# Early modulation weights on whole rows, write-outs of turned x behind them, and another order of late chunks in the feed-forward head

## The reference

```python
cs  = silu(c)                              # c: one row for the prompt, one for the sample
mod = cs @ w_mod + b_mod                   # w_mod: 2048 x 12288
sh_a, sc_a, gt_a, sh_f, sc_f, gt_f = split(mod, 6)
h = rmsnorm(x, g_attn) * (1 + sc_a) + sh_a
z = h @ w_in                               # queries, keys, values of two groups of heads
o = concat(differential_attention(z), sliding_window_attention_with_sinks(z))
x = x + gt_a * (o @ w_out)
h2 = rmsnorm(x, g_ffn) * (1 + sc_f) + sh_f
u = conv3(h2 @ w_up) + conv_b              # causal, depthwise, w_up: 2048 x 11264
gate, val = split(u, 2)
x = x + gt_f * ((silu(gate) * val) @ w_down)
y = rmsnorm(x, g_final)
```

## Time and profile before

| | |
|---|---|
| median of three runs | 2729.01 us |
| profiled execution | 2726.82 us |
| its span | 2724.7 us |
| PE busy | 2638.6 us, 97% |
| DVE busy | 1632.5 us, 60% |
| ACT busy | 962.2 us, 35% |
| POOL busy | 529.8 us, 19% |
| moved by DMA | 324.93 MB, 307.67 MB of it read from HBM |

### The profile page before, as it was taken

The page is one execution under the profiler, slowest core; times in us unless marked ns, Lnnn a source line. Parts: engine busy times, 40 slices in busy tenths (PEclk is TensorE's granted clock), DMA queues, the critical chain, the costliest instruction groups (busy, mean ns, idle before and its releaser), DMA issues.

```text
span 2724.7 us, 50979 instructions
## 1 busy us (share of the span) xinstructions
PE 2638.6 (97%) x20135; PEld 2462.7 (90%) x20135; DVE 1632.5 (60%) x3210; ACT 962.2 (35%) x1871; POOL 529.8 (19%) x461
## 2 busy tenths in 40 slices
PE   7999999999999999899999999999999999999997
PEld 2258989988988999899999999999999999999997
DVE  1359889884446889865445555545554555455564
ACT  2235666664345335432222222222222222222224
POOL 1037777771012443310000000000000000000003
PEclk9999999999999999999999999999999999999998
DMA  8766555562224654533323222332322233233231
GB/s 277 255 211 180 184 173 183 179 175 63 55 57 136 164 170 136 152 109 94 88 84 94 78 83 89 94 92 80 93 88 78 84 94 93 79 93 91 81 93 69
DMA packets 416208, 324.93 MB, mean 119 GB/s; under 512 B 44410, under 2 KB 360218, under 8 KB 414880
## 3 DMA queue, kind: packets, MB, share of 16 engines
q1 hardware_dynamic: 410032, 302.55, 37.5%
q0 software_dynamic: 5248, 14.56, 1.7%
q10 hardware_dynamic: 688, 4.47, 0.5%
HBM read 307.67 MB, written 14.07 MB: 118 GB/s over the span
## 4 chain that ended last, share of the span: by engine, by line
PE 83%; DVE 7%; DMA 3%; issue 2%; POOL 2%; ACT 2%; SPq 1%; ACTq 0%; DVEq 0%; POOLq 0%
PE ps L1574 24%; PE ps L1576 23%; PE ps L1575 23%; PE ps L1548 4%; DVE late_f L1241 3%; PE ps L1663 2%; PE ps L1629 2%; DMA w_raw<-in_w_out 2%; DMA w_raw<-in_w_mod 1%; POOL oT L699 1%; PE ps L1647 1%; SPq L539 1%; ACT w_hi L795 1%; DVE oT L1241 1%; PE ps L1585 1%
## 5 line engine op out<-in xcount | busy, mean ns | idle before, releaser
L1574 PE MATMUL ps<-x_hi,w_hi 128*128 128x272 f32 (+1 forms) x4480 | 1320.1, 295 | 33.0 <-DVE w_lo L1135 23.7
L1575 PE MATMUL ps<-x_lo,w_hi 128*128 128x272 f32 (+1 forms) x4480 | 1298.1, 290 | 0.0
L1576 PE MATMUL ps<-x_hi,w_lo 128*128 128x272 f32 (+1 forms) x4480 | 1296.1, 289 | 0.0
L1574 PEld LDWEIGHTS ps<-x_hi,w_hi 128*128 128x128 f32 x4480 | 850.5, 190 | 48.2 <-issue 24.1
L1576 PEld LDWEIGHTS ps<-x_hi,w_lo 128*128 128x128 f32 x4480 | 851.9, 190 | 0.0
L1575 PEld LDWEIGHTS ps<-x_lo,w_hi 128*128 128x128 f32 x4480 | 849.6, 190 | 0.0
L795 ACT ACTIVATE w_hi<-w_raw 128x1024 fp32r<-128x1024 f32 x368 | 375.4, 1052 | 1052.0 <-PE ps L1576 904.3
L1135 DVE TENSOR_TENSOR w_lo<-w_raw,w_hi 128x1024 fp32r<-128x1024 f32 x368 | 460.7, 1280 | 344.1 <-ACT w_hi L795 343.7
L1576 PE MATMUL ps<-y_hi,w_lo 128*128 128x272 f32 x1408 | 406.8, 289 | 0.0
L1574 PE MATMUL ps<-y_hi,w_hi 128*128 128x272 f32 x1408 | 406.1, 288 | 0.0
L1575 PE MATMUL ps<-y_lo,w_hi 128*128 128x272 f32 x1408 | 404.5, 287 | 0.0
(11 more groups left out here) (195 smaller groups left out, 2116.7 us busy)
## 6 DMA issues: line engine op xcount, KB each, us to landing
w_raw<-in_w_mod SPq DMA_DIRECT2D x192, 512.0 KB, 4.5
w_raw<-in_w_up SPq DMA_DIRECT2D x176, 512.0 KB, 4.6
w_raw<-in_w_down SPq DMA_DIRECT2D x88, 512.0 KB, 4.0
w_raw<-in_w_in SPq DMA_DIRECT2D x56, 512.0 KB, 3.9
w_raw<-in_w_in SPq DMA_DIRECT2D x32, 256.0 KB, 3.7
w_raw<-in_w_out SPq DMA_DIRECT2D x16, 512.0 KB, 5.4
w_raw<-in_w_out SPq DMA_DIRECT2D x64, 128.0 KB, 4.0
x_transposed<-xT SPq DMA_DIRECT2D x4, 1088.0 KB, 7.3
```

The lines of the kernel that those rows point to most:

```text
L1574: pe.matmul(out[:, 0:n], hi_w, hi_x, start=first, stop=False)
L1575: pe.matmul(out[:, 0:n], hi_w, lo_x, start=False, stop=False)
L1576: return pe.matmul(out[:, 0:n], lo_w, hi_x, start=False, stop=last)
```

## The change

Four things are changed in the first 250 us, and one in the feed-forward head.

1. An early k step is one matmul on all 128 rows into one bank. `mod_rows` has 512 columns instead of 1024, and `group_columns` turns them by four transposes instead of eight accumulating matmuls.
2. The transposes of x use two pairs of banks in turn, so a block waits for the copy of the block two before it. The scaled x goes into a tile of its own, hT, instead of back into xT.
3. The four write-outs of turned x stand behind the early weights in SP's queue: blocks 8 to 15 first, in the middle of the first late chunks and w_in chunks (`X_OUT`). Their semaphore is split in two. VectorE, ScalarE and POOL wait for blocks 8 to 15 at late chunk 0, whose sums lie in that memory; ScalarE waits for blocks 0 to 7 at the first attention output, and POOL for all ahead of `x_back`. The earlier waits of VectorE and POOL for all four are gone.
4. The transposes of bias rows use another place in TensorE's memory (columns from 2048 instead of from 1024; not in the diff below).
5. In the feed-forward head, the chunks of w_up that come next stand ahead of late chunks in the programs of VectorE and ScalarE, and in STREAM: `HEAD_LATE` gives, for each step, how many late chunks stand ahead of `evict(0)` and how many behind `conv(0)`: 0 and 3, 1 and 3, 1 and 4, 4 and 0.

```diff
@@ -267,18 +267,21 @@
-HEAD_LATE = {}
-for _j in range(GRP):
-    for _q in range(2):
-        HEAD_LATE[_j, _q] = [LATE1 + LATE2 + 4 * _j + 2 * _q + _i for _i in range(2)]
+HEAD_LATE = []
+_n = LATE1 + LATE2
+for _first, _then in ((0, 3), (1, 3), (1, 4), (4, 0)):
+    HEAD_LATE.append((range(_n, _n + _first), range(_n + _first, _n + _first + _then)))
+    _n += _first + _then
+assert _n == LATE1 + LATE2 + LATE3
 STREAM += [("w", FC0 + _n) for _n in range(4)]
 for _j in range(GRP):
-    for _q in range(2):
-        if _j:
-            STREAM.append(("w", FC0 + 4 * _j + 2 + _q))
-        STREAM += [("mod", _n) for _n in HEAD_LATE[_j, _q]]
+    if _j:
+        STREAM += [("w", FC0 + 4 * _j + 2), ("w", FC0 + 4 * _j + 3)]
+    STREAM += [("mod", _n) for _n in HEAD_LATE[_j][0]]
     if _j + 1 < GRP:
         STREAM += [("w", FC0 + 4 * _j + 4), ("w", FC0 + 4 * _j + 5)]
+    STREAM += [("mod", _n) for _n in HEAD_LATE[_j][1]]
+X_OUT = {EC + 4: 2, EC + 6: 3, EC + 8: 0, EC + 10: 1}
 RAW_OF = {x: r for r, x in enumerate(STREAM)}
...
@@ -341,12 +344,16 @@
+        hT = on(st0, "hT", [P, KT, T])
-        mod_rows = [on(st0, f"mod_rows{i}", [2, 2 * EG]) for i in range(2)]
+        mod_rows = [on(st0, f"mod_rows{i}", [2, EG]) for i in range(2)]
...
@@ -495,11 +503,11 @@
                 slot = r % NR
-                q = (r - X_AT - NR - 5) // 4
-                if r % 4 == 1 and 0 <= q < 4:
-                    sp.wait_ge(xt_ev, 4 * q + 4)
+                if r in X_OUT:
+                    q = X_OUT[r]
+                    sp.wait_ge(xt_ev, KT)
                     sp.dma_start(scratch[4 * q:4 * q + 4].rearrange("k p t -> p k t"), xT[:, 4 * q:4 * q + 4, :]
-                                 ).then_inc(scratch_out, 16)
+                                 ).then_inc(scratch_out[q // 2], 16)
                 if r >= NR:
...
@@ -691,6 +698,8 @@
                     pool.wait_ge(x_ok, 2 * KT)
+                if n == 0:
+                    pool.wait_ge(scratch_out[1], 32)
                 pool.wait_ge(late_act, n + 1)
...
@@ -733,6 +742,8 @@
             pool.wait_ge(t_score, len(TURNS))
+            for x in scratch_out:
+                pool.wait_ge(x, 32)
             x_back(0)
...
@@ -803,7 +814,7 @@
                 for a, c, g in ((0, TP, 0), (TP, TS, 1)):
-                    ins = act.activation(x_hi[:, kt, a:a + c], xT[:, kt, a:a + c], ACT.Identity,
+                    ins = act.activation(x_hi[:, kt, a:a + c], hT[:, kt, a:a + c], ACT.Identity,
                                          bias=mod[:, SH_A + kt, g:g + 1])
...
@@ -812,13 +823,13 @@
                     act.wait_ge(e_t, g - 1)
-                act.activation(mod_rows[g % 2][:, :], bank(6 - 2 * (g % 2), 2)[0:2, :], ACT.Copy).then_inc(e_ev, 1)
+                act.activation(mod_rows[g % 2][:, :], bank(7 - g % 2)[0:2, :], ACT.Copy).then_inc(e_ev, 1)
...
                 act.wait_ge(xt_t, kt + 1)
-                b = bank(0, 2)[:, 0:T]
+                b = bank(2 * (kt % 2), 2)[:, 0:T]
                 if kt >= 2:
...
@@ -848,6 +859,8 @@
                 act.wait_ge(ld_raw[RAW_OF[x] % NR], LOADED[x])
+                if n == 0:
+                    act.wait_ge(scratch_out[1], 32)
                 if n >= 2:
...
@@ -890,6 +903,8 @@
                     act.wait_ge(t_ot, OUT_COUNT[pp])
+                    if OUT_COUNT[pp] == 1:
+                        act.wait_ge(scratch_out[0], 32)
                     if TURNS[pp][0] >= KT - 8:
...
@@ -1001,19 +1016,18 @@
                 act.wait_ge(u_done, J * 4 + 1)
+                late = ((), ()) if has_down else HEAD_LATE[jj]
                 if not first:
-                    for q in range(2):
-                        hi_ffn(at(2 + q))
-                        if not has_down:
-                            for n in HEAD_LATE[jj, q]:
-                                late_mul(n)
+                    hi_ffn(at(2))
+                    hi_ffn(at(3))
+                for n in late[0]:
+                    late_mul(n)
                 act.wait_ge(u_done, J * 4 + (3 if first else 2))
-                if first:
-                    for n in HEAD_LATE[0, 0] + HEAD_LATE[0, 1]:
-                        late_mul(n)
                 hi_ffn(at(4))
...
                 add_shift(0, J)
+                for n in late[1]:
+                    late_mul(n)
                 act.wait_ge(u_done, J * 4 + 4)
...
@@ -1141,7 +1155,7 @@
                 for st in range(2):
-                    ins = dve.tensor_tensor(mod[:, t0:t0 + EGT, st], bank(2)[:, st:2 * EGT:2],
+                    ins = dve.tensor_tensor(mod[:, t0:t0 + EGT, st], bank(5)[:, st:2 * EGT:2],
                                             cols[:, BT, t0:t0 + EGT], ALU.add)
...
@@ -1151,7 +1165,7 @@
                 for a, c, g in ((0, TP, 0), (TP, TS, 1)):
-                    ins = dve.scalar_tensor_tensor(out=xT[:, kt, a:a + c], in0=xT[:, kt, a:a + c],
+                    ins = dve.scalar_tensor_tensor(out=hT[:, kt, a:a + c], in0=xT[:, kt, a:a + c],
                                                    scalar=mod[:, SC_A + kt, g:g + 1], in1=n0_rstd[:, a:a + c],
...
@@ -1160,7 +1174,7 @@
                 for a, c, g in ((0, TP, 0), (TP, TS, 1)):
-                    ins = dve.scalar_tensor_tensor(out=x_lo[:, kt, a:a + c], in0=xT[:, kt, a:a + c],
+                    ins = dve.scalar_tensor_tensor(out=x_lo[:, kt, a:a + c], in0=hT[:, kt, a:a + c],
                                                    scalar=mod[:, SH_A + kt, g:g + 1],
...
@@ -1227,6 +1240,8 @@
                 dve.wait_ge(ld_raw[RAW_OF[x] % NR], LOADED[x])
+                if n == 0:
+                    dve.wait_ge(scratch_out[1], 32)
                 if n % LPG == 0 and g >= 2:
...
@@ -1432,19 +1447,18 @@
                 first = isinstance(J, int) and J == 0
+                late = ((), ()) if has_down else HEAD_LATE[jj]
                 if not first:
-                    for q in range(2):
-                        lo_ffn(at(2 + q))
-                        if not has_down:
-                            for n in HEAD_LATE[jj, q]:
-                                late_sum(n)
+                    lo_ffn(at(2))
+                    lo_ffn(at(3))
+                for n in late[0]:
+                    late_sum(n)
                 evict(0, J)
-                if first:
-                    for n in HEAD_LATE[0, 0] + HEAD_LATE[0, 1]:
-                        late_sum(n)
                 lo_ffn(at(4))
...
                 conv(0, J, c_gate)
+                for n in late[1]:
+                    late_sum(n)
                 evict(1, J)
...
@@ -1525,10 +1539,8 @@
                 for t in range(EGT):
-                    for u in range(2):
-                        mm = pe.matmul(bank(2)[:, 2 * t:2 * t + 2],
-                                       mod_rows[g % 2][0:2, EG * u + P * t:EG * u + P * t + P], ident[0:2, 0:2],
-                                       start=u == 0, stop=u == 1)
+                    mm = pe.transpose(bank(5)[:, 2 * t:2 * t + 2], mod_rows[g % 2][0:2, P * t:P * t + P],
+                                      ident[0:2, 0:2])
                 mm.then_inc(e_t, 1)
...
@@ -1543,10 +1555,8 @@
                     kt = EK * (e % EPG) + k
-                    for u in range(2):
-                        r = slice(64 * u, 64 * u + 64)
-                        mm = pe.matmul(bank(6 - 2 * (g % 2) + u)[0:2, :], cs[r, kt, :],
-                                       w_raw[raw][r, EG * k:EG * k + EG], start=kt == 0, stop=kt == KT - 1)
+                    mm = pe.matmul(bank(7 - g % 2)[0:2, :], cs[:, kt, :], w_raw[raw][:, EG * k:EG * k + EG],
+                                   start=kt == 0, stop=kt == KT - 1)
                 mm.then_inc(m_used, 1)
...
@@ -1558,9 +1568,9 @@
                         pe.wait_ge(ld_x, 16 * (QT + 1))
-                    if kt >= 1:
-                        pe.wait_ge(xt_ev, kt)
-                    b = bank(0, 2)
+                    if kt >= 2:
+                        pe.wait_ge(xt_ev, kt - 1)
+                    b = bank(2 * (kt % 2), 2)
                     for t in range(QT):
...
                     pe.transpose(b[:, TP:T], x_nat[QT][0:TS, P * kt:P * kt + P], ident[0:TS, 0:TS]).then_inc(xt_t, 1)
```

More of the change, by code:

```diff
@@ L343, in build @@
         st0 = ExitStack()
+        rows_st = ExitStack()
+        rows = on(rows_st, "rows", [P, 9, P])
+        rows_st.close()
+        hT = on(st0, "hT", [P, KT, T])
+        n0_acc = on(st0, "n0_acc", [P, T])
         xT = on(st0, "xT", [P, KT, T])
         n0_sq = [on(st0, f"n0_sq{i}", [P, T]) for i in range(2)]
-        n0_acc, n0_rstd = on(st0, "n0_acc", [P, T]), on(st0, "n0_rstd", [P, T])
+        n0_rstd = on(st0, "n0_rstd", [P, T])
         lam = [on(st0, f"lambda{i}", [P, A_DK]) for i in range(4)]
-        mod_rows = [on(st0, f"mod_rows{i}", [2, 2 * EG]) for i in range(2)]
-        rows = on(st0, "rows", [P, 9, P])
+        mod_rows = [on(st0, f"mod_rows{i}", [2, EG]) for i in range(2)]
         st0.close()
@@ L430, in build @@
         B6, B7 = bank(6), bank(7)
```

(9 more changed lines are left out.)

## The result

Beside each other on one chip, the changed kernel took 2707.09 us (median of four runs, 2706.24 to 2707.79) and the kernel before 2728.65 us (2725.24 to 2736.15): a ratio of 0.9917, 95% interval 0.9901 to 0.9932. That is 21.6 us faster; the forecast was 2711, its sum 16.5 us.

The account below looks back on a forecast made before the run. TensorE was taken as the bound (83% of the span), VectorE nearly so in the feed-forward head. Terms 4.8 + 10.8 + 0.9 - 1.0 + 1.0 = 16.5 us gave 2710.3 or 2712.5, taken as 2711; range 2702 to 2722 us.

Parts of the forecast that it names:

- Part 1: Early weights: one tile of 128 rows instead of two 64-row halves saves 24 switches of 0.20 us, 4.8 us.
- Part 2: Turn of modulation rows: four transposes at 0.52 us instead of 1.87 us, eight times, gain 10.8 us.
- Part 3: ScalarE's copies ahead of each turn: 512 instead of 1024 columns, on the chain twice, gain 0.9 us.
- Parts 4 and 5: Two bank pairs for x transposes and own h tile gain nothing; moved write-outs cost 0 (rival: 7 us, chance 0.10).
- Part 6: Early weights: DMA as next bound stalls the four-slot ring; 1 us charged, bounds 0 and 6.2; rival at bound, chance 0.20.
- Part 7: Feed-forward head: VectorE's last late chunk sets the end, TensorE's wait moves; gain 1 us, bounds -3 and +8.5; +8.5 rival, 0.06.

## Why the prediction was right, and where its steps were not

The time was inside the range and the sign was right. How near it came is in part luck: one term of 4.8 us did not come, and gains that the sum did not have took its place. The terms, one by one:

- **Part 1 (4.8 us) failed.** The 0.20 us were there, but not for the halves: they belong to the change from 2 to 128 columns of weights, which the kernel makes at the same places as before. The same L1519 pair stood once behind 2 columns of weights and once behind 128, and I read that as halves against whole rows. The rows on weight loads show both differences (64x2 against 128x128); I used one. The x step, which was to fall to 2.35 us, stayed at 2.57. That whole rows cost nothing either was right (13.82 us for 32 records, 0.43 each), and so was setting the row against the rule of the Trainium skill's "TensorE: Matmul & The Clock Gate", Part 3, The mechanism: in runs of early tiles no load stands in the open, not even with 128 columns.
- **Part 2 had the mechanism, and its size was low.** 8 x 1.53 = 12.2 us instead of 10.8. Four transposes take 0.34, 0.085 each; I had taken 0.13 from transposes of bias rows.
- **Part 3 was right**: 0.43 + 0.41 us.
- **Parts 4 and 5 were right**: the second pair of banks gave nothing, and the write-outs are free at both places as far as the runs can tell.
- **Part 6 charged 1 us that did not come.** A group takes 13.82 us without a stall; the one wait for a load ahead of the last tiles is 3.0 us, where before there were two, of 0.6 and 3.1.
- **Part 7 was right in its mechanism.** No wait at w chunk 4, one at chunk 6, the stage 0.9 us longer instead of 1 shorter. That VectorE bounds it, and POOL's adds set VectorE's pace, is shown by the two experiments that take POOL's adds out of the head. That behind the convolution they slow the convolution instead is shown by its rows (789 to 1245 ns).
- **The clock was missing from the sum.** Two stretches at half clock went with the long turns, 1.7 us each here, and up to 6.3 us together with all turns long. A third, near 65 us, went by chance, and one at 150 us came. Net 3.4 us, with the 1.4 us that part 2 had too little, filled the place of part 1's 4.8 us.
- **The upper end of the range was added up wrongly.** Without part 1's 4.8 us and with half of part 6's bound, 3.1 us instead of 1, the sum is 9.6 us, not 7, which ends the range at about 2719 instead of 2722. The measured time is inside either.

Up to the first main products the profile's account is 12.2 (turns) + 0.84 (copies) + 0.64 (start) + 0.8 (loads) + 1.7 (clock: two stretches gone, near 65 and 107 us, and one new at 150 us) = 16.2 of 16.89 us. Of these the start and the stretch near 65 us are chance. Then 1.7 us come with the stretch near 230 us, and 1.2 us in small steps up to the second sum of squares, of which no single cause was found.

## What to carry to other kernels

Here a turn of 1.9 us behind a pause of TensorE cost 1.7 us more than its own time: look at the granted clock in the stretch behind it, and price the operation with what follows. When one row is dearer than another of the same line, list all that differs in what stood ahead, and not only what the change touches. Where a helper engine slows the one that bounds a stage, moving its work within the stage moves the loss; giving the bound engine the work itself can be cheaper: here twice 749 ns cost nearly the same as once 1388 to 1530 ns beside the helper, and the engine's other work got its speed back.

## What the runs showed of the hardware that was not expected

- A weight load of 128 columns did not start under a matmul with 2 columns of weights (0.20 us in the open at the first sum of squares), and did under one with 128. The Trainium skill's "TensorEngine Tiling (Array Packing)", Tiling Modes, Key Properties, says that changing the tiling mode drains TensorE; the 1.06 and 0.86 us agree with it, if 2 columns count as a narrower mode, which no run here shows directly.
- VectorE's multiply-add takes 749 ns alone and up to 1.79 us beside POOL's adds; one of the convolution's takes 789 ns alone and 1245 on average beside them. The Trainium skill's "SBUF — State Buffer", SBUF: two separate sides, says that an instruction of VectorE with two inputs from SBUF and one of GpSimd that reads SBUF want the same pair of ports, that whichever starts first holds it for the whole instruction, and that the other waits. Products that take up to 1.04 us longer beside adds of 1.28 to 1.75 us agree with that.
